# Sample copies as whole-array transposes, rounded pairs of products for sums of squares, and three zero fill weights

## The reference

```python
# layer 0: gated DeltaNet (8 heads of 128) beside GLA (4 heads, keys 128, values 256)
u = rmsnorm(h) @ ab_w_in; qkv = silu(causal_conv(u[qkv]))
q = l2norm(q) * 128**-0.5; k = l2norm(k)        # a sum of squares over 128 per head and token
o_dn = rmsnorm(gated_delta(q, k, v, beta, g, state)) * silu(z)
o_gla = rmsnorm(gla(gq, gk, gv, glog, state)) * silu(z_gla)   # a sum over 256
h += concat(o_dn, o_gla) @ ab_w_out
# layer 1: Mamba-2 SSD (16 heads of 64, 4 groups) beside RG-LRU (1024 channels)
y_ssd = rmsnorm over 256 of ((ssd(c, b, x * dt, g, state) + d * x) * silu(z))
h += concat(y_ssd, y_lru) @ cd_w_out
# after each layer
h += sigmoid(rmsnorm(h) @ W_gate[i]) * (p[i] @ W_proj[i])
```

## Time and profile before

| | us |
|---|---|
| median of 3 runs (2417.98 to 2419.77) | 2419.04 |
| the profiled execution, its own time | 2417.75 |
| its span, first to last instruction | 2415.8 |
| PE busy (98% of the span) | 2378.8 |
| DVE busy (54%) | 1297.6 |
| ACT busy (40%) | 970.1 |
| POOL busy (15%) | 369.8 |

### The profile page before, as it was taken

One profiled execution on the slowest core, in us unless ns is written; L12 is line 12 of the kernel. 1 busy time (PEld: TensorE's weight loads), 2 busy tenths in 40 slices (PEclk: granted clock), 3 DMA queues, 4 the chain that ended last, 5 costly groups with the idle time before them and its releaser, 6 DMA issues.

```text
span 2415.8 us, 50483 instructions
## 1 busy us (share of the span) xinstructions
PE 2378.8 (98%) x21567; PEld 2271.0 (94%) x21567; DVE 1297.6 (54%) x2426; ACT 970.1 (40%) x1579; POOL 369.8 (15%) x553
## 2 busy tenths in 40 slices
PE   7999999999999999999999999999999999999998
PEld 7999999989999999899999999988899999999998
DVE  6755656565654564632344466466657572234445
ACT  5523444323444344432342253334445562234335
POOL 3101101111101001011111112122212121111111
PEclk9999999999999999999999999999999999999999
DMA  9433333333343453552233343233323345323335
GB/s 240 114 99 115 114 99 118 95 105 108 109 120 111 141 152 114 190 187 88 84 95 113 102 116 94 71 89 94 85 81 105 87 151 171 88 84 95 89 91 164
DMA packets 389807, 275.88 MB, mean 114 GB/s; under 512 B 24739, under 2 KB 359341, under 8 KB 389072
## 3 DMA queue, kind: packets, MB, share of 16 engines
q1 hardware_dynamic: 358256, 187.74, 28.2%
q0 software_dynamic: 19520, 62.29, 8.3%
q10 hardware_dynamic: 11808, 22.63, 2.6%
HBM read 224.96 MB, written 48.37 MB: 113 GB/s over the span
## 4 chain that ended last, share of the span: by engine, by line
PE 57%; ACT 1%; DVE 1%; DMA 0%; issue 0%; ACTq 0%; DVEq 0%
PE psd L612 50%; PE psw L634 2%; PE psw L633 1%; PE psw L1000 0%; PE psw L1039 0%; PE psw L711 0%; PE psw L992 0%; PE psw L980 0%; ACT arena L1307 0%; DVE arena L1897 0%; ACT w_hi L1181 0%; PE psw L697 0%; PE psw L703 0%; PE psw L1089 0%; DMA mix<-yT_scratch 0%
## 5 line engine op out<-in xcount | busy, mean ns | idle before, releaser
L612 PE MATMUL psd<-xh,w_hi 128*128 128x272 f32 (+2 forms) x5056 | 1108.8, 298 | 4.7 <-DVE w_lo L1754 2.9
L612 PE MATMUL psd<-xl,w_hi 128*128 128x272 f32 (+2 forms) x5056 | 1058.1, 289 | 3.6 <-DVE xl L1816 2.6
L612 PE MATMUL psd<-xh,w_lo 128*128 128x272 f32 (+2 forms) x5056 | 1055.4, 288 | 0.0
L612 PEld LDWEIGHTS psd<-xh,w_hi 128*128 128x128 f32 x5056 | 798.8, 189 | 55.6 <-issue 37.2
L612 PEld LDWEIGHTS psd<-xl,w_hi 128*128 128x128 f32 x5056 | 795.9, 189 | 4.7 <-DVE xl L1816 3.5
L612 PEld LDWEIGHTS psd<-xh,w_lo 128*128 128x128 f32 x5056 | 800.1, 189 | 0.0
L1754 DVE TENSOR_TENSOR w_lo<-w_raw,w_hi 128x512 fp32r<-128x512 f32 x648 | 447.4, 712 | 360.6 <-ACT w_hi L1181 359.4
L1181 ACT CAST w_hi<-w_raw 128x512 fp32r<-128x512 f32 x648 | 385.5, 615 | 552.0 <-PE psd L612 467.6
L2676 POOL TENSOR_TENSOR states<-states,extra 128x544 f32<-128x544 f32 x45 | 67.8, 1508 | 467.1 <-ACT extra L1236 466.9
L2455 DVE TENSOR_TENSOR extra<-psd,rstd 128x544 f32<-128x544 f32 (+2 forms) x36 | 23.8, 661 | 142.0 <-PE psd L612 125.0
L2426 DVE TENSOR_TENSOR arena<-arena,psd 128x544 f32<-128x544 f32 x32 | 23.0, 720 | 131.9 <-PE psd L612 128.0
(11 more groups left out here) (516 smaller groups left out, 2395.3 us busy)
## 6 DMA issues: line engine op xcount, KB each, us to landing
w_raw<-in_ab_w_in_dram SPq DMA_DIRECT2D x224, 256.0 KB, 3.0
w_raw<-in_cd_w_in_dram SPq DMA_DIRECT2D x148, 256.0 KB, 3.1
w_raw<-in_ple_w_gate_dram SPq DMA_DIRECT2D x144, 256.0 KB, 3.2
w_raw<-in_ab_w_out_dram SPq DMA_DIRECT2D x64, 256.0 KB, 2.9
w_raw<-in_cd_w_out_dram SPq DMA_DIRECT2D x64, 256.0 KB, 2.9
uT_scratch<-mix ACTq DMA_DIRECT2D x53, 272.0 KB, 2.3
hT_scratch<-arena POOLq DMA_DIRECT2D x8, 1088.0 KB, 6.3
raws<-uT_scratch POOLq DMA_DIRECT2D x12, 544.0 KB, 4.4
```

What stands on the lines that cost most here:

```text
L612: mm = pe.matmul(out[:, at_c:at_c + ts.stop - ts.start], w[:, r, k % QH, :], x[:, k, ts], start=(k == 0 and i == 0), stop=(k == KT - 1 and ...
```

## The change

`sums` replaces the plain product with ones by two rounded ones, of a rounded copy of the squares (`hi`) and of the rest (`lo`). ACT writes the rounded copy, DVE the rest (`lo_of_sums`). `silu_squares` of the next head moves ahead of `rstd_of` on ACT. `sample_copies` makes the copies by transposes of the last 128, 96, 64 and 32 columns, each over the one before; DeltaNet `kt` and SSD `xt`, `bts` make two copies and no longer four. `sP` multiplies with 128 weight columns. `sb1`, `ys` and `o` get the fill weight 0, so that no dense slice stands ahead of them.

```diff
-FILL = {... ("dn", "ssq"): 8.0, ... ("ssd", "n"): 1.75, ...}
+FILL = {... ("dn", "ssq"): 7.0, ("dn", "n"): 2.0, ... (("ssd", 7), "n"): 1.75, ("ssd", "n"): 2.6, ...
+        ("gla", "sb1"): 0.0, ("ssd", "ys"): 0.0, ("ssd", "o"): 0.0}
...
+            def sums(W, hi, lo):
+
+                all_tokens(W, onesR[:, :], hi, start=True, stop=False, skip_group_check=True)
+                return all_tokens(W, onesR[:, :], lo, start=False, stop=True, skip_group_check=True)
...
+            def sample_copies(W, src, copies):
+
+                for j in range(copies, 0, -1):
+                    mm = pe.transpose(W[0:NS * j, 0:P], src[:, T - NS * j:T], ident[:, :])
                 return mm
 
             def to_token_major(W, src, copies=1):
 
                 for t in range(NT):
                     pe.transpose(W[:, P * t:P * t + P], src[:, P * t:P * t + P], ident[:, :])
-                if copies == 4:
-                    return four_times(W[:, SEQ:SEQ + P], src[:, SEQ:T], ident[:, :])
-                return pe.transpose(W[0:NS, SEQ:SEQ + P], src[:, SEQ:T], ident[:, :])
+                return sample_copies(W[:, SEQ:SEQ + P], src, copies)
...
                 W = group(u, "ssq")
-                pe.wait_ge(S["dn_sq"], h + 1)
-                all_tokens(W, ones[:, :], slot(6), start=True, stop=True).then_inc(S["work_ready"], 1)
+                pe.wait_ge(S["sum_lo"], lo_count(u, "ssq"))
+                sums(W, slotR(12), slotR(6)).then_inc(S["work_ready"], 1)
                 W = group(u, "ssk")
-                all_tokens(W, ones[:, :], slot(7), start=True, stop=True).then_inc(S["work_ready"], 1)
+                sums(W, slotR(13), slotR(7)).then_inc(S["work_ready"], 1)
...
                 W = group(u, "kt")
-                to_token_major(W, k, copies=4).then_inc(S["work_ready"], 1)
+                for t in range(NT):
+                    pe.transpose(W[:, P * t:P * t + P], k[:, P * t:P * t + P], ident[:, :])
+                pe.transpose(W[:, SEQ:SEQ + P], slot(1, w=SEQ - NS + P)[:, SEQ - NS:], ident[:, :])
+                pe.transpose(W[0:NS, SEQ:SEQ + P], k[:, SEQ:T], ident[:, :]).then_inc(S["work_ready"], 1)
...
                 W = group(u, "n")
-                pe.wait_ge(S["dn_osq"], h + 1)
-                all_tokens(W, ones[:, :], osq, start=True, stop=True).then_inc(S["work_ready"], 1)
+                pe.wait_ge(S["sum_lo"], lo_count(u, "n"))
+                sums(W, slotR(8), slotR(4)).then_inc(S["work_ready"], 1)
...
-                    mm = pe.matmul(W[hp, P * t:P * t + P], Bt[:, t, SSD_N * g:SSD_N * (g + 1)], v2[:, P * t:P * t + P],
+                    mm = pe.matmul(W[:, P * t:P * t + P], Bt[:, t, P * (g // 2):P * (g // 2) + P], v2[:, P * t:P * t + P],
...
# silu_squares on ACT
+                if h == 0:
+                    act.wait_ge(S["h_stored"], 64)
+                act.activation(slot(6, 2), slot(0, 2), ACT.Square)
+                act.activation(slotR(12, 2), slot(0, 2), ACT.Square).then_inc(S["dn_sq"], 1)
# dn on ACT
                 W = group(u, "o")
-                act.activation(slot(4), W[:, 0:T], ACT.Square).then_inc(S["dn_osq"], 1)
+                act.activation(slot(4), W[:, 0:T], ACT.Square)
+                act.activation(slotR(8), W[:, 0:T], ACT.Square).then_inc(S["dn_osq"], 1)
+                if h + 1 < DN_H:
+                    silu_squares(h + 1)
                 W = group(u, "n")
                 rstd_of(W, slot(3), 1.0 / P, 3 * h + 3, S["dn_rstd"], S["dn_ln"])
-                if h + 1 < DN_H:
-                    silu_squares(h + 1)
# gla on ACT; ssd the same with stageR[:, 1, :] and stage[:, 0, :]
+                act.wait_ge(S["pair_sum"], h + 1)
+                act.copy(slotR(10), slot(9)).then_inc(S["sum_hi"], 1)
# DVE
+            def lo_of_sums(s, sR, hiR):
+
+                dve.tensor_tensor(sR, s, hiR.bitcast(F32), ALU.subtract).then_inc(S["sum_lo"], 1)
+
+            def pair_lo(h):
+
+                dve.wait_ge(S["dn_sq"], h + 1)
+                lo_of_sums(slot(6, 2), slotR(6, 2), slotR(12, 2))
...
                                          ALU.mult).then_inc(S["dn_o1"], 1)
+                lo_of_sums(slot(4), slotR(4), slotR(8))
                 skip(u, "n")
+                if ahead:
+                    pair_lo(h + 1)
                 dve.wait_ge(S["dn_rstd"], h + 1)
# gla on DVE, ahead of sb0; in ssd the same after L2336, ahead of skip(u, "n")
+                dve.wait_ge(S["sum_hi"], h + 1)
+                lo_of_sums(slot(9), slotR(9), slotR(10))
```

More of the change, by code:

```diff
@@ L203 @@
 bc_conv bc_silu bc_b bc_cb
-sp_conv sp_silu sp_D sp_ebc sp_A sp_v sp_um sp_s sp_gs sp_snew sp_i sp_o sp_y sp_sq pair_sum sp_ln sp_rstd sp_out
+sp_conv sp_silu sp_D sp_ebc sp_A sp_v sp_um sp_s sp_gs sp_snew sp_i sp_o sp_y sp_sq pair_sum sum_hi sum_lo sp_ln sp_rstd sp_out
 lr_conv lr_r lr_i lr_a lr_t lr_sq lr_hs lr_y
@@ L239, in trunk @@
         xh, xl = sb("xh", [P, KT, T], F32R), sb("xl", [P, KT, T], F32R)
-        arena = sb("arena", [P, KT * T])
+        with nc.sbuf_tensor("arena", [P, KT * T], F32) as arena:
+            pass
+        arenaR = sb("arenaR", [P, KT * T], F32R)
         KH = KT // 2
@@ L252, in trunk @@
         stage = mix[:, 3 * T:5 * T].rearrange("p (e t) -> p e t", e=2)
+        stageR = mixR[:, 3 * T:5 * T].rearrange("p (e t) -> p e t", e=2)
         extra = sb("extra", [P, 4 * T])
@@ L260, in trunk @@
         ident, ones = sb("ident", [P, P]), sb("ones", [P, P])
+        onesR = sb("onesR", [P, P], F32R)
         cb16 = sb("cb16", [P, 14 * P + P + P + 32 + T + 8 * 32 + 8], BF16)
@@ L294, in slot, with slotR, lo_count @@
             return arena[:, T * i:T * i + n * w]
+        def slotR(i, n=1):
+            return arenaR[:, T * i:T * i + n * T]
+        def lo_count(u, name):
+            kind, h = u
+            if kind == "dn":
+                return 2 * h + (2 if name == "n" else 1)
+            return 2 * DN_H + (h + 1 if kind == "gla" else GLA_H + h // 2 + 1)
         def ssd_x(p):
@@ L682, in four_times @@
                 for j in range(4):
-                    mm = pe.matmul(W[32 * j:32 * j + 32, 0:rhs.shape[-1]], samples, rhs, **(kw or dict(start=True, stop=True)))
+                    mm = pe.matmul(W[32 * j:32 * j + 32, 0:rhs.shape[-1]], samples, rhs, **kw)
+                return mm
+            def sample_copies(W, src, copies):
+                for j in range(copies, 0, -1):
+                    mm = pe.transpose(W[0:NS * j, 0:P], src[:, T - NS * j:T], ident[:, :])
                 return mm
@@ L729, in columns_of_rows @@
                 st = slot(4)
-                for t in range(NT):
-                    pe.transpose(W[:, P * t:P * t + P], st[:, P * t:P * t + P], ident[:, :])
-                four_times(W[:, SEQ:SEQ + P], st[:, SEQ:T], ident[:, :]).then_inc(S["work_ready"], 1)
+                to_token_major(W, st, copies=4).then_inc(S["work_ready"], 1)
             def one_row(h, beta=0):
@@ L932, in gla @@
                 W = group(u, "n")
-                pe.wait_ge(S["pair_sum"], h + 1)
-                all_tokens(W, ones[:, :], slot(9), start=True, stop=True).then_inc(S["work_ready"], 1)
+                pe.wait_ge(S["sum_lo"], lo_count(u, "n"))
+                sums(W, slotR(10), slotR(9)).then_inc(S["work_ready"], 1)
             def bc():
@@ L946, in bc @@
                 for i in range(2):
-                    mm = four_times(W[:, P * i:P * i + P], slot(i)[:, SEQ:T], ident[:, :])
+                    mm = sample_copies(W[:, P * i:P * i + P], slot(i), 2)
                 mm.then_inc(S["work_ready"], 1)
@@ L975, in ssd @@
                 pe.wait_ge(S["sp_silu"], p + 1)
-                to_token_major(W, xs, copies=4).then_inc(S["work_ready"], 1)
+                to_token_major(W, xs, copies=2).then_inc(S["work_ready"], 1)
                 W = group(u, "sP")
@@ L1005, in ssd @@
                     W = group(u, "n")
-                    pe.wait_ge(S["pair_sum"], GLA_H + p // 2 + 1)
-                    all_tokens(W, ones[:, :], stage[:, 0, :], start=True, stop=True).then_inc(S["work_ready"], 1)
+                    pe.wait_ge(S["sum_lo"], lo_count(u, "n"))
+                    sums(W, stageR[:, 1, :], stageR[:, 0, :]).then_inc(S["work_ready"], 1)
             def lru(j):
@@ L1476, in ssd @@
                 if e:
+                    act.wait_ge(S["pair_sum"], GLA_H + p // 2 + 1)
+                    act.copy(stageR[:, 1, :], stage[:, 0, :]).then_inc(S["sum_hi"], 1)
                     W = group(u, "n")
@@ L1960, in rows_ab @@
                 go(dve.memset(slot(11), 0.0))
+                go(dve.tensor_copy(onesR[:, :], ones[:, :]))
                 for r in (slice(32, 64), slice(64, 128)):
@@ L2022, in dn @@
                         dn_conv(0, tap, samples=True)
+                    pair_lo(0)
                 for n in ("ssq", "ssk", "gbc"):
@@ L2336, in ssd @@
                     dve.tensor_tensor(stage[:, 0, :], stage[:, 0, :], stage[:, 1, :], ALU.add).then_inc(S["pair_sum"], 1)
+                    dve.wait_ge(S["sum_hi"], GLA_H + p // 2 + 1)
```

(1 more changed line is left out.)

5 lines of the change are left out of this document (2 added, 3 removed).

## The result

The changed kernel takes 2427.87 us (median of 5 runs, 2426.44 to 2429.38), the kernel before 2419.04 beside it: a ratio of 1.0036, 95% interval 1.0024 to 1.0048. Predicted were 2400 and a range of 2388 to 2411. The profiled execution has a span of 2427.2 us where the one before had 2415.8.

The account below looks back on a forecast made before the run. TensorE, busy 2378.8 of 2415.8 us, was taken as the bound. Its stream shortens by 30.1 us, less waits of 4.9, 4.7 and 1.4, so 19.1 off 2419.04 gives 2400; range 2388 to 2411.

Parts of the forecast that it names:

- The work: TensorE's stream: sums 13.4, copies 7.1, `sP` 2.5, `sb0` with `sb1` 5.0, other side-by-side groups 2.1; 30.1 us less.
- the overlap: GLA's `sb0` and `sb1` on different rows run at once, both costing 1.25 us and not 2.50; 5.0 us saved.
- the delay of 0.43: By strict start and end order, `sb0`'s late half would hold `sb1` back some 0.43 us, losing 1.7 of 5.0.
- What is late next: New TensorE waits at DeltaNet `n` (4.9), SSD `ys` (4.7) and SSD `n` (1.4 us), taken off the saving.
- `n` of DeltaNet: Waits 0.7 us in heads 1 to 7 for two squares, L2125 and the subtraction on DVE; 4.9 us in all.
- `ys`: SSD's `ys` waits for `sp_s`: 0.9 in pairs 1 and 3, 2.0 more in pair 5; 4.7 us with `sP`'s 0.9.
- DVE has its time: SSD even pairs and pair 7: `xt` moves three slices later, so no added wait was counted there.
- the 0.9 at `sP`: SSD: shorter `xt` brings `sP`, already waiting for DVE, 0.3 us sooner; 3 x 0.3 of added waits.
- its chain ahead of `sb0`: nothing: GLA's `n` stands five slices after `sb1` with its chain ahead of `sb0`; no wait counted.
- Hidden, with 2.2 us to spare: DeltaNet `ssq`: inputs ready at 261.1, TensorE reaches it at 263.3 us, so no wait.
- slower by the wait at `ssq`: Rival, chance 0.04: DeltaNet's `ssq` becomes the wait in seven heads; at a chain 6 us later, 2427 us.
- Waits twice as long: Rival, chance 0.20: in-order DVE with `w_lo` and evictions between the links doubles the forecast waits; about 2411 us.

Follow-up runs that it names:

- the three runs above: Kernel before with ten unneeded TensorE waits added to its dense stream: gaps of 0.98, 1.73 and 2.48 us gave 2430.66, 2440.51 and 2455.06 us.
- weights alone: Kernel before with only the change's fill weights, so groups stand at other dense slices and no instruction differs: 2436.21 us, ratio 1.0062.
- DeltaNet's slots back: Changed kernel with DeltaNet's weights set to `ssq` 8, `n` 2, `o` 2, giving its groups their earlier slices again: 2416.81 us, ratio 0.9993.
- `sb1` at 1.0: Changed kernel with only the fill weight of GLA's `sb1` put back from 0 to 1.0: 2424.22 us, ratio 1.0018.
- the second round: Changed kernel with all three head kinds' slices given back, then head 0's `ssq`, GLA head 3's `qk` and pair 5's `ss`, `ys` moved later: 2404.2 us, 0.994.

## Why the prediction was wrong

**The work: right.** 30.1 us were to leave TensorE's stream; the account shows 28.1, and the groups' own rows add up to about 30. The 2 us between can be what the waits cost beyond their gaps (0.2 to 0.3 each in the three runs above); that was not separated. The sums (0.51 for 0.49), `kt` (0.66), `sP` (0.90) and the overlap (1.27 for 1.25) all stand in rows. On the overlap two ideas stood against each other: full, or the second pair held back. The trace has all four groups of 32 rows in 1.27 us, so nothing of `sb1` is held back. The Trainium skill, TensorE: Matmul & The Clock Gate, The mechanism, says that products start and end strictly in order. The trace agrees: of the eight records four start from 783.55 to 783.57 and four from 784.08 to 784.10, with their ends in the same order. Wrong was the delay of 0.43 that I had worked out from it; such an order leaves room for full overlap.

**What is late next: this step failed.** It stood in the prediction as 4.9 + 4.7 + 1.4 = 11.0 us of waits, and what it named came at about that size: `n` of DeltaNet waits 0.50 in seven heads (0.7 predicted), `ys` 5.0 (4.7), SSD's `n` 0.8 (1.4). At `ys` part of the agreement is luck. Pairs 1, 3 and 5 wait 0.7, 0.8 and 2.5, near the forecast, but 1.0 comes in pair 7, where "DVE has its time" was wrong: there, too, `ys` now stands three slices behind `sP` and no longer six. And the 0.9 at `sP` did not come; its waits fell from 1.4 us to 0.1, with `xt` and `sP` a slice later in the changed kernel. What failed is that I looked for late inputs only at groups whose *inputs* the change touches, and put every other group at nothing. 26.5 us came, and the larger part stands at groups whose code did not change:

- *`vt`, 7.0 us.* A group takes one of two PSUM buffers and so waits for the reader of the group two back, here DVE's product after `qk`, some 7 us behind `kk`. `ssq` 8 to 7 moved `kk` from slice 183 to 182 and `vt` from 188 to 186: five slices became four, by rounding. `kk`, DVE's product and `vt` of head 1:

```profile
203.38 1.20 PE L669 MATMUL psw<-arena 128*128 128x128 f32 x10
...
209.83 0.16 DVE L2096 TENSOR_TENSOR arena<-psw,arena 32x32 f32<-32x32 f32 x1
210.05 0.66 PE L715 MATMUL psw<-ident,arena 128*128 128x128 f32 x4 [0.61 <-DVE arena L2096]
```

The kernel with weights alone has 4.6 us of this wait, the one with DeltaNet's slots back 2.0. The other 2.4 fit `kt`'s saving of 0.33 in seven heads, which comes back as a wait here.
- *`qk` of GLA, 7.1 us.* The zero weight of `sb1` did not bring `sb1` to `sb0` but `sb0` to `sb1`: 767 to 771, with all the head before it up to four slices later, while the next `qk` stayed at 784. The decay scan of the next head on DVE and two exponentials on ACT follow the state's update and stand ahead of ACT's `rstd` and of the product `qk` reads. Before head 3, the scan (L1956), the second exponential, `rstd`, the product and `qk`:

```profile
968.21 1.29 DVE L1956 TENSOR_TENSOR_SCAN arena<-cb,arena 128x544 f32<-128x544 bf16 x1
...
970.36 0.66 ACT L1414 ACTIVATE arena<-arena 128x544 f32<-128x544 f32 x1 [0.17 <-DVE arena L1962]
...
976.50 0.66 ACT L1247 ACTIVATE arena<-arena 128x544 f32<-128x544 f32 x1
977.07 0.64 ACT L1421 ACTIVATE raws<-raws 128x544 f32<-128x544 f32 x1
977.85 1.57 PE L659 MATMUL psw<-raws 128*128 128x128 f32 x8 [4.22 <-ACT raws L1421]
```

The prediction counted `n` there ("its chain ahead of `sb0`: nothing"), and never asked who follows `sb0`. The kernel with weights alone waits 5.9 us here, the one with `sb1` at 1.0 only 0.6. I had done this very reckoning for SSD, from the planner's positions, and not for GLA.
- *`x6`, 1.9 us, and the decay groups, 2.4 us*: the same slice lost in DeltaNet. Weights alone give all of `x6`'s wait and 0.5 us of the other. With the sums the decay groups wait 2.4, and with DeltaNet's slots back neither is among the waits, so the second takes both the lost slice and the new sums. The two sums ahead of it are 0.4 us cheaper each, which brings it forward; that this is the missing part was not tried alone.
- *`ssq` of head 0, 2.2 us.* "Hidden, with 2.2 us to spare" was worked out for heads 1 to 7, and there it held. Head 0 was reckoned only for the stores it might wait for, and those do not hold it up. But there the second square (1.1 us) and the subtraction (1.3) stand directly between `silu` and TensorE. At the same slice 81 the wait is 0.9 to 2.2 us in different kernels; two slices later than in the kernel before, in the second round, there is none.

**The clock: not in the prediction at all.** Every wait was priced at its own length. Some 20 us more at half clock cost 10.2 us by the account (9 at the 1.5 measured for 3.4 us), nearly as much as all waits that were forecast.

The rival "slower by the wait at `ssq`", chance 0.04, gave 2427, the measured time, by a mechanism that did not happen in any of its seven heads; that agreement is chance. "Waits twice as long", at 0.20, had the nearest reason, yet still gave 2411, because it scaled known waits and had no room for unlooked-for ones. By the prediction's own test ("at DeltaNet `n` ... and `ys` of odd pairs should stand first among PE's new waits") it was wrong: third and fourth.

## What to carry to other kernels

In a stream whose order a planner writes from weights, a changed weight is a change to every group of that unit. List the slices of all groups before and after, and for each look at what it waits for, its buffer's last reader included; a weight of zero moves the earlier group to the later one. When an instruction gets cheaper, the weights have to be set again: the same code was 9 us slower than before at one set of slices and 15 us faster at another. What waits are left should be short: ten gaps of 2.48 us cost 36 us, nearly half as much again as their length, ten of 0.98 us 11.7.

## What the runs showed of the hardware

- A gap on TensorE costs more than itself, and long ones can lower its granted clock from 2.4 to 1.2 GHz (PEclk 1.00 to 0.50): in one profiled execution each, after 0 of 10 gaps of 0.98 us, 1 of 10 of 1.73 and 6 of 10 of 2.48, each time for 3.4 us, at a cost of 1.5 us. In the kernels of this study such stretches were also 6.8 and 10.2 us long, and in a few cases came after gaps of 0.8 to 1.0 us.
- The spread of a kernel's time from run to run goes with this clock: the same program, `sb1` at 1.0, has spans of 2415.8 to 2426.6 us with mean clocks of 0.996 to 0.991.
- Four groups of 32 rows at 512 columns overlap fully on TensorE: 1.27 us for four where two take 1.25.
